# A hybrid decoder layer on one core: RMSNorm sums spread by a matrix of ones in place of columns that are turned back by an identity

## The reference

```python
def rmsnorm(x, g):
    y = xf * lax.rsqrt(jnp.mean(xf * xf, axis=-1, keepdims=True) + EPS)
    return (y * g.astype(jnp.float32)).astype(x.dtype)
...
    h = rmsnorm(x, g_mix[l]);   ... h @ w_in[l]
    hq = rmsnorm(x, g_mem_q[l]); ... hq @ w_mem_q[l]
    hf = rmsnorm(x, g_ffn[l]);  ... hf @ w_up[l]
```

## Time and profile before

| | |
|---|---|
| time, median of 3 runs | 1843.29 us (1840.32 to 1844.22) |
| profiled execution, its own time | 1844.52 us |
| its span | 1842.8 us |
| busy: TensorE, VectorE, ScalarE, GpSimd | 95%, 64%, 36%, 42% |

### The profile page before, as it was taken

How to read it: one execution, slowest core, us unless ns; L and a number is a source line. 1 busy time by engine, 2 the same in 40 slices (tenths; PEclk the granted TensorE clock), 3 DMA queues, 4 the chain that set the end, 5 groups by cost and what they waited for, 6 DMA issues and landing times.

```text
span 1842.8 us, 23394 instructions
## 1 busy us (share of the span) xinstructions
PE 1745.0 (95%) x8548; PEld 1445.3 (78%) x8548; DVE 1175.5 (64%) x1573; ACT 662.9 (36%) x1206; POOL 774.9 (42%) x575
## 2 busy tenths in 40 slices
PE   7998899989999996989999898999999999999997
PEld 6886788877888885878777687878888888788886
DVE  6754577776877776446343634767777777645554
ACT  4114577875222333134111213444444444211212
POOL 3333344443432331410222243467777777444451
PEclk9997899998999998989999998999999999999999
DMA  5230011010111113115101022022222221744432
GB/s 186 81 115 12 24 35 35 29 42 1 57 46 46 37 43 126 46 37 157 46 23 34 23 103 80 23 103 100 72 92 80 92 81 51 292 147 160 139 137 92
DMA packets 54229, 143.92 MB, mean 78 GB/s; under 512 B 4924, under 2 KB 21500, under 8 KB 54016
## 3 DMA queue, kind: packets, MB, share of 16 engines
q1 hardware_dynamic: 46776, 115.52, 18.9%
q10 hardware_dynamic: 7368, 27.28, 3.8%
HBM read 118.65 MB, written 24.13 MB: 77 GB/s over the span
## 4 chain that ended last, share of the span: by engine, by line
PE 63%; DVE 21%; ACT 7%; issue 5%; POOL 2%; DMA 0%; ACTq 0%; DVEq 0%; SPq 0%; POOLq 0%
PE ps L796 15%; PE ps L800 15%; PE ps L799 15%; DVE x_t L2294 5%; PE ps L975 3%; ACT x_t L1618 2%; DVE x_t L2323 2%; PE ps L1037 2%; PE ps L1110 2%; DVE ps L2286 2%; PE ps L946 2%; POOL sum_s L734 1%; DVE h_lo L1733 1%; PE ps L994 1%; PE ps L1089 1%
## 5 line engine op out<-in xcount | busy, mean ns | idle before, releaser
L677 POOL TENSOR_TENSOR w_hi<-w_raw,ones 128x1024 fp32r<-128x1024 f32 x77 | 155.8, 2023 | 754.1 <-PE ps L796 631.3
L796 PE MATMUL ps<-h_hi,w_hi 128*128 128x512 f32 x1108 | 438.3, 396 | 15.3 <-DVE h_lo L1732 6.2
L800 PE MATMUL ps<-h_hi,w_lo 128*128 128x512 f32 x1108 | 434.7, 392 | 0.0
L799 PE MATMUL ps<-h_lo,w_hi 128*128 128x512 f32 x1108 | 434.4, 392 | 0.0
L796 PEld LDWEIGHTS ps<-h_hi,w_hi 128*128 128x128 f32 x1108 | 210.1, 190 | 65.2 <-issue 8.5
L800 PEld LDWEIGHTS ps<-h_hi,w_lo 128*128 128x128 f32 x1108 | 209.9, 189 | 44.5
L799 PEld LDWEIGHTS ps<-h_lo,w_hi 128*128 128x128 f32 x1108 | 210.2, 190 | 43.7 <-issue 0.7
L680 POOL TENSOR_TENSOR w_lo<-w_raw,w_hi 128x1024 fp32r<-128x1024 f32 x77 | 218.6, 2839 | 6.0
L1732 DVE TENSOR_TENSOR z_lo<-x_t,z_hi 128x1024 fp32r<-128x1024 f32 x44 | 113.0, 2607 | 104.9 <-ACT z_hi L1637 104.9
L705 POOL TENSOR_SCALAR probs<-probs,nsa_inv,gate_sig 128x640 f32<-128x640 f32 (+7 forms) x128 | 100.3, 783 | 176.8 <-DVE nsa_inv L1936 176.7
L2294 DVE SCALAR_TENSOR_TENSOR x_t<-ps,par,x_t 128x1023 f32<-128x1023 f32 x84 | 107.7, 1283 | 71.7 <-ACT x_t L1618 70.2
(11 more groups left out here) (316 smaller groups left out, 3480.6 us busy)
## 6 DMA issues: line engine op xcount, KB each, us to landing
w_raw<-in_w_tiles SPq DMA_DIRECT2D x131, 512.0 KB, 3.7
x_t<-z_dram SPq DMA_DIRECT2D x44, 512.0 KB, 5.1
z_dram<-x_t ACTq DMA_DIRECT2D x21, 512.0 KB, 2.6
q_st<-q_dram SPq DMA_DIRECT2D x64, 128.0 KB, 2.9
x_f<-in_x_rows SPq DMA_DIRECT2D x8, 512.0 KB, 9.0
x_t<-in_x_rows ACTq DMA_DIRECT2D x1, 4096.0 KB, 13.3
x_dram<-x_t ACTq DMA_DIRECT2D x8, 512.0 KB, 2.6
x_res<-x_dram SPq DMA_DIRECT2D x2, 2048.0 KB, 10.3
```

The costliest lines, as they stand in the source:

```text
L677: pool.tensor_tensor(w_hi[s][:, :], w_raw[s][:, :], ones[:, :].to_broadcast([P, KT * P]), ALU.mult).then_inc(w_hi_made.sem, w_hi_made.up())
L796: ins = mm(out_ap, whi, x_hi, start=first, stop=False)
L799: mm(out_ap, whi, x_lo, start=False, stop=False)
L800: return mm(out_ap, wlo, x_hi, start=False, stop=last)
```

## The change

The stationary operand of the sum is now a 128x128 matrix of ones (the column of ones, broadcast), and the accumulated squares move past it 512 tokens at a time, in float32. Every row of PSUM banks 6 and 7 then holds the sum of each token. ACT takes the root from there on 128x1024 into `r_in` or `r_bc`, and DVE inverts it there in place. The column tiles, the identity products of `spread_roots` and DVE's copies are gone. In the third norm `token_sums` moves behind the first weight tile of the MLP, and ACT's root behind all 16 pieces of `h_hi`.

```diff
-            def token_sums(squares, bank):
+            def token_sums(squares):

                 sq_used.add(2 + KT)
                 pe.wait_ge(sq_used.sem, sq_used.value())
-                for j in range(TT):
-                    last = mm(ps[:, bank, j:j + 1], squares[:, j * P:j * P + P], ones[:, :], start=True, stop=True)
+                for c in range(2):
+                    last = mm(ps[:, 6 + c, :], ones[:, :].to_broadcast([P, P]), squares[:, c * HALF:c * HALF + HALF],
+                              start=True, stop=True)
                 last.then_inc(sums_ready.sem, sums_ready.up())
...
-            token_sums(acc_x, 6)
-            gemm_tile(h_hi, h_lo, after_half=spread_roots)
+            token_sums(acc_x)
+            gemm_tile(h_hi, h_lo)
...
-            token_sums(acc, 4)
-            gemm_loop(KT // 4, 4, hm_hi, hm_lo, MEM)
-            spread_roots()
-            gemm_loop(KT // 4, 4, hm_hi, hm_lo, MEM)
+            token_sums(acc)
+            gemm_loop(KT // 2, 4, hm_hi, hm_lo, MEM)
...
-            token_sums(acc, 4)
             freed_now()
...
             plain_tile(0, 0, each_piece)
-            spread_roots()
+            token_sums(acc)
             plain_tile(0, 1)
...
-            def norm_root():
-                act.wait_ge(col_ready.sem, col_ready.next())
-                f(col[:, :], col[:, :], ACT.Sqrt, scale=1.0 / D, bias=EPS).then_inc(
+            def norm_root(dst):
+                act.wait_ge(sums_ready.sem, sums_ready.next())
+                f(dst[:, :], ps_flat[:, 6 * HALF:6 * HALF + SEQ], ACT.Sqrt, scale=1.0 / D, bias=EPS).then_inc(
                     std_ready.sem, std_ready.up())
...
             split_hi(x_t, 0, KT, G_FFN)
-            norm_root()
             split_hi(x_t, KT, 2 * KT, G_FFN)
+            norm_root(r_bc)
...
-            def columns_end():
+            def norm_end(dst):
                 dve.wait_ge(std_ready.sem, std_ready.next())
-                dve.reciprocal(col[:, :], col[:, :]).then_inc(vector_chain.sem, vector_chain.up())
-                dve.wait_ge(vector_chain.sem, vector_chain.value())
-                dve.tensor_copy(col_r[:, 0, :], col[:, :]).then_inc(vector_chain.sem, vector_chain.up())
-                dve.wait_ge(vector_chain.sem, vector_chain.value())
-                low(col_r[:, 1, :], col[:, :], col_r[:, 0, :]).then_inc(r_col_ready.sem, r_col_ready.up())
...
+                dve.reciprocal(dst[:, :], dst[:, :]).then_inc(vector_chain.sem, vector_chain.up())
                 dve.wait_ge(vector_chain.sem, vector_chain.value())
...
-            columns_start(6)
-            columns_end()
-            copy_spread(r_in[:, :], 6)
+            norm_end(r_in)
...
                 if n == KT - 1:
-                    copy_spread(r_bc[:, :], 6)
+                    norm_end(r_bc)
...
-            dve.wait_ge(spread_ready.sem, spread_ready.next())
-            dve.tensor_copy(r_bc[:, :], ps_flat[:, 6 * HALF:6 * HALF + SEQ]).then_inc(t("r_copied").sem, t("r_copied").up())
+            dve.wait_ge(std_ready.sem, std_ready.next())
+            dve.reciprocal(r_bc[:, :], r_bc[:, :]).then_inc(t("r_copied").sem, t("r_copied").up())
```

More of the change, by code:

```diff
@@ L476, in build @@
                      "xh_loaded gate_done ssq_ready mixed_ready split_ready mem_loaded mem_scaled sq_ready sq_used "
-                     "r_col_ready sums_ready col_ready spread_ready kv_hi_made tap_ready h_ready x_shift_ready "
+                     "sums_ready kv_hi_made tap_ready h_ready x_shift_ready "
                      "x_exp_ready xv_ready conv_done gelu_ready "
@@ L773, in _ @@
             q_loaded, out_copied = [t("q_loaded0", 16), t("q_loaded1", 16)], t("out_copied")
-            r_col_ready, qk_ready, split_ready = t("r_col_ready"), t("qk_ready"), t("split_ready")
-            sums_ready, spread_ready = t("sums_ready"), t("spread_ready")
+            qk_ready, split_ready, sums_ready = t("qk_ready"), t("split_ready"), t("sums_ready")
             sq_used, tile_started, weights_split = t("sq_used"), t("tile_started"), t("weights_split")
@@ L807, in each_piece, with gemm_tile @@
                 pe.wait_ge(h_ready.sem, h_ready.next())
-            def gemm_tile(x_hi, x_lo, width=SEQ, wait_piece=None, skip=0, after_half=None):
+            def gemm_tile(x_hi, x_lo, width=SEQ, wait_piece=None, skip=0):
                 s = next_weights()
                 for c in range(0, width, HALF):
-                    if c and after_half:
-                        after_half()
                     n = min(HALF, width - c)
@@ L1250, in _ @@
             x_exp_ready, x_shift_ready = t("x_exp_ready"), t("x_shift_ready")
-            z_made, col_ready, tap_ready = t("z_made"), t("col_ready"), t("tap_ready")
+            z_made, sums_ready, tap_ready = t("z_made"), t("sums_ready"), t("tap_ready")
             kv_hi_made, tile_started, y_t_ready = t("kv_hi_made"), t("tile_started"), t("y_t_ready")
@@ L1301, in _ @@
                     x_high(k + 2)
-            norm_root()
+            norm_root(r_in)
             def high_keys(br):
@@ L1701, in _ @@
             block_high, block_low = t("block_high"), t("block_low")
-            r_col_ready, split_ready = t("r_col_ready"), t("split_ready")
+            split_ready = t("split_ready")
             sq_ready, sq_used, ssq_ready = t("sq_ready"), t("sq_used"), t("ssq_ready")
-            std_ready, col_ready, sums_ready = t("std_ready"), t("col_ready"), t("sums_ready")
-            spread_ready, tap_ready = t("spread_ready"), t("tap_ready")
+            std_ready, tap_ready = t("std_ready"), t("tap_ready")
             vector_chain, x_exp_ready, x_split = t("vector_chain"), t("x_exp_ready"), t("x_split")
```

14 lines of the change are left out of this document (removed).

## The result

The changed kernel takes 1863.37 us (median of 4 runs, 1861.86 to 1864.75) against 1843.24 for the kernel before in the same comparison (4 runs, 1840.32 to 1844.22): a ratio of 1.0122 with an interval of 1.0106 to 1.0137. It is slower, and by 11 us more than predicted; 1863.4 lies outside the range of 1845.5 to 1857. Its profiled execution took 1863.26 us with a span of 1861.5, 18.7 more than the span before.

A forecast was written before the change was run, and what follows sets the result against it. TensorE was read as busy 95% of the span, with stretches at VectorE's pace. The three norms' -0.75 + 5.2 + 4.3 = +8.75 us, on 1843.3, gave 1852 us, range 1845.5 to 1857.

The forecast's parts named there:

- rival D: Pauses at the second norm and at p = 2 and 3 lengthen TensorE's half clock: 3 to 6 us more; chance 0.15.
- Reciprocal 6.55 us: VectorE's reciprocal at 1024 columns, extrapolated from three narrow widths: 6.55 us, bounds 1.2 and 6.8.
- Root 1.01: The root on 128x1024 out of PSUM takes 1.01 us, by a square of the same shape.
- First norm, -0.75: First norm: scalings start 0.75 us earlier and TensorE gains the same; the spread's other 1 us becomes a wait.
- Second norm, +5.2: Second norm: reciprocal delays tile 10's low half 3.9 us, TensorE waits some 5; with clock loss +5.2 us (3.3 to 8).
- Third norm, +4.3: Third norm: later gain's products and VectorE's turns with GpSimd delay the MLP's remaining products by 4.3 us (0 to 6).
- +0.8: Third norm: ACT's root waits for sums behind TensorE's first tile, so the gain's products start 0.8 us later.
- The collisions: Third norm: VectorE's differences and low halves take turns with GpSimd's splits; included in the +4.3 us there.
- A (no collisions): Collisions with GpSimd fall as before, no clock loss either: +3.7 to +5 us, 1847 to 1848; chance 0.2.
- B (fast reciprocal): Wide reciprocal runs at the copy's pace, 1.2 us: -2.5 to +1 us, 1841 to 1844; chance 0.07.
- C (slack in the chain): After the third norm TensorE sets the pace, earlier `h_lo` reaches the end: -3 to -5 us, near 1839; chance 0.06.

The follow-up runs named there:

- 32 bytes put back: The changed kernel with 32 unused bytes put ahead of the reused part of SBUF; 1856.82 us, ratio 1.0092 to the kernel before.
- everything moved alike: The changed kernel with all tiles 32 bytes up and the reused ones 128, all distances between operands multiples of 128; 1844.82 us, ratio 1.0018 to the kernel before.
- the 96 bytes kept: The changed kernel with 96 unused bytes ahead of the reused part of SBUF; 1849.22 us, ratio 1.0054 to the kernel before.

## Why the prediction was wrong

The failed step is one that stands in no sentence of the sum: it priced the norms and took every other instruction to last as long as before. The diff drops `col` and `col_r`, and that I read as tiles gone, not as tiles moved. What the runs showed in its place: TensorE's matmuls of 1234 us and later, which the diff doesn't touch, started every 230.0 and 234.2 ns in place of 226.7, and that is the 13 us; 96 unused bytes took them back. The chances show the same: the end of rival D, 1858, was the highest time I allowed for, and no rival had a mechanism outside the norms.

- **New operations.** Reciprocal 6.55 us: measured 6.55. The estimate from the Trainium skill ("VectorE: DVE Perf Modes", First, the fixed hardware budget), 8.5 us from a repeat count of 8, doesn't fit; the rows give 6.4 ns a column. Root 1.01: 1.03.
- **First norm, -0.75.** The scalings start at 44.60 instead of 46.23. The changed kernel had started 0.99 earlier already (its first `h_lo` at 8.66 us, before 9.65; the kernel before with 32 bytes more did that too, so it isn't the change), so the norm gave -0.6, and TensorE's pause for `kvp` was 1.0 us, as predicted. One pair of executions can't show a term this small, since the eleven other kernels with the old norm stand at -1.4 to +0.2 in this stretch; but the mean of the eight with the new norm (-1.55) is 0.7 below that of the twelve with the old one (-0.86). Right.
- **Second norm, +5.2.** Tile 10's low half 3.8 late (predicted 3.9), a pause of TensorE of 4.9 (predicted 5), the clock below full in it. The whole was +5.07. In the other kernels that keep the reciprocal there it was between 4.7 and 6.5, and in those with the old norm between -0.3 and +2.4; the two means (5.7 and 0.9) are 4.8 apart. Right, and shown by moving the reciprocal out of the loop.
- **Third norm, +4.3.** Measured +2.3. The gain's products started at 1159.50, 3.27 later than before, on a mark that was 3.24 late: +0.0 where I had +0.8. The collisions: differences +1.5 (15.57 against 14.05), first pair of low halves +2.2, second +1.7, third -3.1 (2.35 instead of 5.44), together +2.3 where I serialised to +3.5. The mechanism was right, its size 2 us too large. Two of the six kernels with this norm (32 bytes put back; everything moved alike) lost 3.9 instead: their root waited 9.19 us for the sums where the others waited 7.6, with a mean granted clock of 0.66 from 1146 to 1151 us in the first of them, so part of TensorE's first tile ran at 1.2 GHz later in the tile than elsewhere, and the gain's products came 1.6 late. The prediction also misread one row: the seventh difference ended 1.1 us behind GpSimd's `w_lo`; 0.09 is the gap to the next one. TensorE's wait for `p_sum` went from 2.5 us to 3.8.
- **Sum of the norms.** -0.6 + 5.07 + 2.3 = +6.8 in the profiled execution, and +9.3 by the medians with the 96 bytes kept, against +8.75 predicted. The interval of the latter is 6 to 14 us, so that it lies so near 8.75 is in part luck.
- **The rest.** From +5.6 behind the third norm to +18.7 at the end: 3.3 ns for each of the 1596 matmuls of the seven products is 5.3 us, 7.5 ns for each of the 1056 of the down products is 7.9, together 13.2.
- **Rivals.** A (no collisions), B (fast reciprocal) and C (slack in the chain) didn't come about. Of D (more clock) the pauses came, but not the cost: the granted clock fell twice more than before, in the windows of 1193 to 1197 and 1227 to 1234 us, both of which had 1.00 before,

```profile
1193.00:1197.00 4.00, 3.87 (x10) 3.09 (x11) 4.00 (x3) 1.60 (x2) 3.02 (x2) 0.57 0.01 4
1227.00:1234.00 7.00, 4.94 (x12) 3.88 (x13) 3.40 (x3) 5.03 (x8) 5.19 (x5) 0.52 0.42 150
```

while the scalings stayed 5.6 us late from 1205 to 1250 us, and the 13 us were lost at a granted clock of 1.00.

## What to carry to other kernels

When a change drops or resizes a tile in a memory laid out by a running offset, list what moves behind it and keep the places, or count matmuls per microsecond in stages that the change doesn't touch: a TensorE that is fully busy can still be 3% slower. A long operation on an engine that feeds a loop without slack can cost most of its length (some 5 of 6.55 us here), and nothing a few microseconds later; look for the nearest place where that engine waits. And of two engines that take turns, the one that starts earlier can save more than its lead: here 7.6 us for 3.85.

## What the runs showed of the hardware

The spacing of float32 matmuls of 512 columns, each with its own weight load, isn't fixed at full clock: it was 226.7 to 234.2 ns with where the moving operand lay to the stationary one, modulo 256 bytes. The Trainium skill ("TensorE: Matmul & The Clock Gate", Step-by-step: what each phase is for) says that the two operands have independent read ports and that loading the next weights takes no read bandwidth from the running matmul. At seven of eight places of `z` a matmul with its weight load took 2.1 to 7.5 ns more than 226.7 here; whether the load or something else took them no run shows. On an operand's place the skill ("SBUF — State Buffer", Operand start alignment) asks for a multiple of the element size and says that this is about legality, not speed; all places tried here are such multiples. A read conflict between the two ports would fit the rows, but was only argued, and the fast 0 of `h` beside the slow 0 of `z` says that it isn't the whole of it.

A 128x1024 reciprocal in place takes 6.55 us on VectorE, 6.4 ns a column, in all three places, two of them beside GpSimd's splits (37.24 to 41.60 and 1158.85 to 1163.22 us).
